# A grouped mixture-of-experts decoder kernel: the tokens' rows are gathered for two expert pairs at a time, between the weight units of gate and up, instead of for four pairs at once

## What is computed

```
def grouped_moe(h, w_router, router_bias, w_gate, w_up, w_down):
    scores = jax.nn.sigmoid((hf @ w_router).astype(jnp.float32))
    ...
    gates = jnp.sum(jax.nn.one_hot(expert_ids, N_EXPERTS, dtype=jnp.float32) * w_sel[..., None], axis=1)
    out = jnp.zeros_like(hf)
    for e in range(N_EXPERTS):
        y = (jax.nn.silu(hf @ w_gate[e]) * (hf @ w_up[e])) @ w_down[e]
        out = out + gates[:, e:e + 1] * y
    return out.reshape(b, s, d)
```

## Time and profile before

| | us |
|---|---|
| median of 3 runs | 651.88 (651.45 to 651.89) |
| span of the profiled execution, first to last instruction | 650.5 |
| device time around that span, if it is one of the runs shown | 1.0 to 1.4 |
| PE busy | 635.9 (98%) |
| PE's weight loads busy | 344.4 (53%) |
| DVE busy | 311.2 (48%) |
| ScalarE busy | 195.1 (30%) |
| GpSimd busy | 134.6 (21%) |
| loads of the weight ring (queue q1) | 234.46 MB, 85.4% of 16 DMA engines over the span |
| the 1024 matmuls of gate and up (L694) | 223.6 |
| the 512 of down (L715) | 113.8 |

### The profile page before, as it was taken

How to read it: one execution, slowest core, us unless ns; L and a number is a source line. 1 busy time by engine, 2 the same in 40 slices (tenths; PEclk the granted TensorE clock), 3 DMA queues, 4 the chain that set the end, 5 groups by cost and what they waited for, 6 DMA issues and landing times.

```text
span 650.5 us, 7970 instructions
## 1 busy us (share of the span) xinstructions
PE 635.9 (98%) x3227; PEld 344.4 (53%) x3227; DVE 311.2 (48%) x600; ACT 195.1 (30%) x389; POOL 134.6 (21%) x125
## 2 busy tenths in 40 slices
PE   8999999999999999999999999999999999999993
PEld 5887886453333443333488878764433344333431
DVE  6598997622033020320678989893032040320326
ACT  5832963240010221110193377351210032110111
POOL 1899300700000000000049960042000000000000
PEclk9999999999999999999999999999999999999998
DMA  8991299899999999999996118999999999999991
GB/s 360 433 391 66 102 430 428 358 434 422 430 426 426 432 425 427 427 427 429 427 426 297 50 66 316 430 368 418 429 431 424 430 426 425 430 424 431 427 391 67
DMA packets 18330, 240.79 MB, mean 370 GB/s; under 512 B 2032, under 2 KB 2160, under 8 KB 3440
## 3 DMA queue, kind: packets, MB, share of 16 engines
q1 hardware_dynamic: 17136, 234.46, 85.4%
q10 hardware_dynamic: 1152, 5.77, 2.2%
HBM read 239.17 MB, written 1.05 MB: 369 GB/s over the span
## 4 chain that ended last, share of the span: by engine, by line
PE 87%; DMA 5%; DVE 5%; issue 1%; ACT 1%; DVEq 0%
PE bank L694 31%; PE bank L715 16%; PE bank L586 13%; PE bank L743 5%; PE bank L560 5%; DMA ring<-in_units 5%; PE bank L667 2%; PE bank L805 2%; PE bank L817 2%; PE bank L647 2%; DVE w_split L1395 1%; PE bank L627 1%; PE bank L574 1%; PE bank L704 1%; PE bank L887 1%
## 5 line engine op out<-in xcount | busy, mean ns | idle before, releaser
L694 PE MATMUL bank<-ring,xe 128*64 128x512 f32 x1024 | 223.6, 593 | 0.6 <-DMA ring<-in_units 0.6
L694 PEld LDWEIGHTS bank<-ring,xe 128*64 128x64 f32 x1024 | 74.5, 137 | 143.1 <-issue 139.8
L715 PE MATMUL bank<-ring,area_b 128*64 128x512 f32 x512 | 113.8, 596 | 0.2
L1598 DVE TENSOR_TENSOR area_b<-area_b,bank 128x512 f32<-128x512 f32 x16 | 11.0, 688 | 209.4 <-PE bank L694 209.4
L1215 POOL TENSOR_TENSOR rstd<-var_eps,half_neg 128x1 f32<-128x1 f32 x18 | 10.6, 592 | 467.3 <-DVE var_eps L1327 467.3
L1248 POOL TENSOR_TENSOR in_lo<-ring,in_hi 128x512 fp32r<-128x512 f32 x56 | 71.2, 1328 | 13.6 <-ACT in_hi L1015 13.6
L715 PEld LDWEIGHTS bank<-ring,area_b 128*64 128x64 f32 x512 | 35.2, 137 | 66.7 <-issue 64.9
L1618 DVE SCALAR_TENSOR_TENSOR y_lo<-bank,slot_gate,y_hi 128x512 fp32r<-128x512 f32 x32 | 24.0, 751 | 85.0 <-ACT y_hi L1108 85.0
L1094 ACT ACTIVATE area_b<-bank 128x512 f32<-128x512 f32 x16 | 9.6, 597 | 163.8 <-PE bank L694 163.8
L1108 ACT ACTIVATE y_hi<-bank,slot_gate 128x512 fp32r<-128x512 f32 x32 | 22.0, 687 | 96.3 <-PE bank L715 96.3
L1675 DVE SCALAR_TENSOR_TENSOR bank<-mix,small,bank 128x256 f32<-128x256 f32 x116 | 45.6, 484 | 0.0
(11 more groups left out here) (204 smaller groups left out, 797.0 us busy)
## 6 DMA issues: line engine op xcount, KB each, us to landing
ring<-in_units SPq DMA_DIRECT2D x109, 2048.0 KB, 23.2
ln_par<-in_ln_rows ACTq DMA_DIRECT2D x4, 1024.0 KB, 8.4
ring<-in_units SPq DMA_DIRECT2D x2, 1024.0 KB, 8.2
h<-in_x SPq DMA_DIRECT2D x2, 512.0 KB, 4.2
piece_area<-in_branch_rows ACTq DMA_DIRECT2D x2, 512.0 KB, 5.5
ln_par<-in_ln_rows SPq DMA_DIRECT2D x1, 1024.0 KB, 36.1
piece_area<-in_sgw_cols ACTq DMA_DIRECT2D x2, 256.0 KB, 5.8
out<-h SPq DMA_DIRECT2D x1, 512.0 KB, 2.7
```

Of the source, the lines that this page charges most:

```text
L694: mm = pe.matmul(bank[2 + m][e * SLOTS:(e + 1) * SLOTS, :], xe[:, k, at + e * SLOTS:at + (e + 1) * SLOTS], w[:, c, m, e, :], start=k == 0, ...
L715: mm = pe.matmul(bank[5 + n][e * SLOTS:(e + 1) * SLOTS, :], hidT[:, k, e * SLOTS:(e + 1) * SLOTS], w[:, k, e, :], start=k == 0, stop=k == ...
```

## The change

`GROUP` goes from 4 to 2: all gathers are for two pairs (256 columns), so a layer has four of them, of 32 matmuls each. Two chunks share a PSUM bank.
- The first (`first_pairs`) stands where `first_pair` stood.
- The others stand inside the second pair of the group before (j = 1, 3, 5): chunks 0-1, 2-3 and 4-5 after the first, second and third unit of gate and up, chunks 6-7 inside down, ahead of its second unit.
- `combine` uses four banks (7, 4, 3 and 0 or 1), so its second half no longer waits for the first half's additions; it waits for those of the pair before.
- `turn_pick` moves ahead of `turn_hid`.
- On DVE the copy of `hidT` moves ahead of all four additions, and `picks` for the next group moves to the even pairs.
- The loads keep their order, their ring of 9 slots and their waits (the experts' third unit waits for the same count as the second, behind which it stands anyway).
- Tiles in `area_a` and `area_b` move; the `more` version follows.

The core of the diff:

```diff
-GROUP = 4
+GROUP = 2
-REST_BANKS = (1, 4, 7, 3, 1, 4, 7, 0)
-GROUP_BANKS = (2, 3, 0, 1, 4, 7, 0, 1)
-GATHERS = {"main": (3 * KC, 3 * TB), "more": (KC, TB)}
+NEXT_BANKS, MORE_BANKS = (0, 7, 4, 7), (0, 1, 7, 4)
+CHUNK_PAIRS = KC // 2
+GATHERS = {"main": (ITERS, ITERS), "more": (1, 1)}
-COMB_BANKS, LAST_COMB_BANKS = (7, 4, 7, 4), (7, 4, 2, 3)
+COMB_BANKS, LAST_COMB_BANKS = ((7, 4, 3, 0), (7, 4, 3, 1)), (7, 4, 2, 3)
...
+                def gather(g, p):
+
+                    dst = bank[(NEXT_BANKS if ps.main else MORE_BANKS)[p]]
+                    for c in (2 * p, 2 * p + 1):
+                        half = slice(c % 2 * GROUP * P, (c % 2 + 1) * GROUP * P)
                         for b in range(TB):
+                            wait_pick(g, b)
                             for part in (n_hi, n_lo):
+                                mm = pe.matmul(dst[:, half], part[:, b, c * P:(c + 1) * P], pick[:, b, :],
+                                               start=c % 2 == 0 and b == 0 and part is n_hi, stop=b == TB - 1 and part is n_lo,
+                                               skip_group_check=True)
+                    mm.then_inc(s["gathered"], 1)
...
                 def turn_pick(j):
 
                     nth("pick_w", j)
+                    if j >= 2:
+                        added(j - 2, 4)
...
                     for u in range(4):
-                        if j % GROUP == 0 and u == 2 and not (ps.main and j == 0):
-                            gather(g, range(4, KC))
...
+                            if j % GROUP == 0 and m == 0:
+                                wait_xe(g, k + 1)
+                            if j >= 2 and k == 0 and m == 1:
+                                added(j - 2, 3)
...
                         mm.then_inc(ps.used, 1)
+                        if gathers_next(j) and u < CHUNK_PAIRS - 1:
+                            if u == 0:
+                                nth("back", j - 1)
+                            elif j >= 2:
+                                added(j - 2, u)
+                            gather(g + 1, u)
...
                             if ps.main and j == pairs - 1 and n == 1 and k == 2:
                                 combine(j, (0, 1))
+                            if gathers_next(j) and n == 1 and k == 0:
+                                added(j - 1, 1)
+                                gather(j // GROUP + 1, CHUNK_PAIRS - 1)
...
-                        banks = LAST_COMB_BANKS if ps.main and j == pairs - 1 else COMB_BANKS
-                        if banks[k] == COMB_BANKS[k] and k >= 2:
-                            added(j, k - 1)
-                        elif k < 2 and j:
-                            added(j - 1, k + 3)
+                        banks = LAST_COMB_BANKS if ps.main and j == pairs - 1 else COMB_BANKS[j % 2]
+                        if k < 2 and j:
+                            added(j - 1, k + 1)
+                        if k < 2 and j + 1 < pairs and gathers_next(j + 1):
+                            wait_xe(j // GROUP + 1, 4 + 2 * k)
...
                     gate_up(j)
-                    if j == 0 and ps.main:
-                        other_pairs((0,))
-                        turn_pick(0)
-                        turn_hid(0)
-                        other_pairs((1,))
-                    elif j == 0:
-                        turn_pick(0)
-                        turn_hid(0)
-                    else:
+                    if j:
                         combine(j - 1, (0, 1))
-                        turn_hid(j)
+                    turn_pick(j)
+                    turn_hid(j)
+                    if j:
                         combine(j - 1, (2, 3))
-                        turn_pick(j)
                     down(j)
-                    if j == 0 and ps.main:
-                        other_pairs(range(2, KC))
-                    if (j + 1) % GROUP == 0 and j + 1 < pairs:
-                        gather((j + 1) // GROUP, range(0, 4))
...
+                tokens(0, range(CHUNK_PAIRS))
                 for j in range(pairs):
+                    gathers_next = ps.main and j % GROUP == GROUP - 1 and j + 1 < pairs
+                    if gathers_next:
+                        tokens(j // GROUP + 1, range(CHUNK_PAIRS - 1))
                     nth("gate_done", j)
                     act.activation(silu, bank[2][:, :], ACT.Silu).then_inc(s["silu"], 1)
...
                                        scale=slot_gate[:, j % 2:j % 2 + 1]).then_inc(s["y_hi"], 1)
+                        if gathers_next and n == 0:
+                            tokens(j // GROUP + 1, (CHUNK_PAIRS - 1,))
...
+                picks(0)
                 if ps.main:
-                    picks(0, 0, 2)
                     normal_low(l, 0)
                     normal_low(l, 1)
-                    picks(0, 2)
...
                     dve.tensor_tensor(hid, silu, bank[3][:, :], ALU.mult).then_inc(s["hid"], 1)
+                    nth("hid_t", j)
+                    dve.tensor_copy(hidT, bank[2][:, :].rearrange("p (c s) -> p c s", c=FC)).then_inc(s["hidT"], 1)
                     if ps.main and j == 1:
                         dve.wait_ge(acc_init, TB * (l + 1))
                     if j:
-                        add_back(j - 1, (0, 1))
-                    nth("hid_t", j)
-                    dve.tensor_copy(hidT, bank[2][:, :].rearrange("p (c s) -> p c s", c=FC)).then_inc(s["hidT"], 1)
-                    if j:
-                        add_back(j - 1, (2, 3))
+                        add_back(j - 1, range(4))
...
                     if j + 1 < pairs:
-                        if (j + 1) % GROUP == 0:
-                            picks((j + 1) // GROUP)
                         weighted_picks(j + 1)
+                        if j % GROUP == 0 and ps.main and j + GROUP < pairs:
+                            nth("pick_w", j + 1)
+                            picks(j // GROUP + 1)
```

More of the change, by code:

```diff
@@ L388, in __init__ @@
                 self.landed = landed_sems
-                self.chunks, self.picks = GATHERS[name]
+                self.gathers, self.picked = GATHERS[name]
         def moe_sems(name):
@@ L629, in first_pair @@
                                            skip_group_check=True)
-                            if b == TB - 1 and part is n_lo:
+                            if b == TB - 1 and part is n_lo and c % 2 == 1:
                                 mm.then_inc(s["gathered"], 1)
[L633 to L642, removed]
+                def gather(g, p):
+                    dst = bank[(NEXT_BANKS if ps.main else MORE_BANKS)[p]]
+                    for c in (2 * p, 2 * p + 1):
+                        half = slice(c % 2 * GROUP * P, (c % 2 + 1) * GROUP * P)
@@ L651, in gather @@
[L651 to L658, removed]
-                            added(GROUP * g - 2, 4)
-                        elif c == (3 if ps.main else 0) and g:
-                            nth("back", GROUP * g - 1)
-                            nth("slot_gate", GROUP * g - 1)
-                        for b in range(TB):
-                            if c == 0:
-                                wait_pick(g, b)
-                            for part in (n_hi, n_lo):
-                                mm = pe.matmul(bank[GROUP_BANKS[c] if ps.main else c % 2][:, :],
-                                               part[:, b, c * P:(c + 1) * P], pick[:, b, :],
-                                               start=b == 0 and part is n_hi, stop=b == TB - 1 and part is n_lo)
-                        mm.then_inc(s["gathered"], 1)
+                                mm = pe.matmul(dst[:, half], part[:, b, c * P:(c + 1) * P], pick[:, b, :],
+                                               start=c % 2 == 0 and b == 0 and part is n_hi, stop=b == TB - 1 and part is n_lo,
+                                               skip_group_check=True)
@@ L748, in experts @@
                 if ps.main:
-                    first_pair(n_hi)
-                    first_pair(n_lo)
-                else:
-                    gather(0, range(0, 4))
+                    first_pairs(n_hi)
+                    first_pairs(n_lo)
+                else:
+                    for p in range(CHUNK_PAIRS):
+                        gather(0, p)
                 for j in range(pairs):
@@ L1100, in experts @@
                        .then_inc(s["slot_gate"], 1)
-                    if ps.main and j == 0:
-                        tokens(0, (1,), 3 * P)
                     nth("slot_gate", j)
```

184 lines of the change are left out of this document (81 added, 103 removed).

## The result

The changed kernel takes 653.25 us (653.18 to 653.6, 8 runs) beside 651.69 (651.45 to 652.47, 8 runs) for the kernel before: ratio 1.0022, 95% interval 1.0012 to 1.0031. It is slower by 1.6 us. The forecast was 653.6, +1.7.

The account below looks back on a forecast made before the run. PE and DMA were taken to bound the experts within a microsecond per layer. PE's +0.07 + 3.45 - 6 x 0.30 = +1.7 at unit 45 became +1.15 and +0.6, together +1.7 on 651.9: 653.6 us, range 651.7 to 656.3.

Parts of the forecast that it names:

- Two limits within a microsecond: In the experts, PE loses only 0.26 and 0.81 us per layer to DMA at unit 45, so both limits nearly coincide.
- Insertions: Gathers placed into gate and up and down: 12 per layer at 0.958 + 0.375 us, net +3.45 us per layer.
- First gather: Ahead of unit 0, 32 matmuls of 256 instead of 128 columns: +0.07 us per layer.
- Middles: From the start of combine to the start of down: -0.30 us for each of seven middles per layer.
- The sum: PE +1.7 us at unit 45; +1.15 in the first layer, +0.6 in the second, together +1.7 us.
- At no cost: Picks, token copies, the additions behind hidT, new bank waits and loads: claimed to cost PE and the DMA stream nothing.
- B: Rival: the middles save only 0.15 us each, total +3.8 us, 655.7 us; chance 0.08.
- C: Rival: a new wait on PE at pairs with a gather, +4 us on top, 657 to 658 us; chance 0.03.
- D: Rival: gather matmuls of 256 columns take 0.14 instead of 0.12 us, +5 us, 658.7 us; chance 0.02.
- A: Rival: DMA stays the limit at unit 45, so not slower, 651.4 to 652.3 us; chance 0.42 with its border.

Follow-up runs that it names:

- before_light: The kernel before with three expert units per layer loaded to one eighth, so less DMA: 650.95 us, ratio 0.9986.
- mids_only: The kernel before with only the changed middles (four combine banks, turn_pick ahead of turn_hid, hidT copy ahead of the additions): 651.53 us, ratio 0.9995.
- mids_light: mids_only with three expert units per layer loaded to one eighth: 646.79 us, ratio 0.9921.
- merged_light: merged with three expert units per layer loaded to one eighth: 649.18 us, ratio 0.9953.
- old_dve: The changed kernel with the first two additions again ahead of the hidT copy on VectorE: 653.34 us, ratio 1.0020.
- old_pe: The changed kernel with turn_pick again behind the second half of combine: 653.13 us, ratio 1.0017.
- old_banks: The changed kernel with combine's two banks, their waits and VectorE's order as before, only turn_pick still ahead: 654.05 us, ratio 1.0027.
- after_light: The changed kernel with three expert units per layer loaded to one eighth: 653.30 us, ratio 1.0022.
- merged: The changed kernel with the three gathers inside gate and up made in a row behind the third unit: 652.09 us, ratio 1.0002.
- merged_early: merged with unit 9 loaded in two halves, the first once PE has used half of unit 0: 653.50 us, ratio 1.0021.

## Why the prediction was right

- **Two limits within a microsecond.** Right in both sizes: the stalls at unit 45 were 0.25 and 0.79 us (before_light), and PE time that comes is seen behind them: +1.63 - 0.25 = +1.38 and +1.63 - 0.79 = +0.84 in the stretches. The same fact made the saving of the middles invisible on the kernel before (mids_only against mids_light). One sentence of the prediction has it the wrong way round: with 3.96 us per unit against 4.93, PE is faster than the stream within the pairs. The stream begins with the ring full, and PE uses up that lead until unit 45.
- **Insertions.** 1.30 measured for 1.33. That the cost lies in the number of switches is shown by merged_light: the same matmuls, 12 switches fewer, -4.1 us, 0.34 out and back. That it is the change of column mode was only argued, as the type of the matmuls changes with it. The Trainium skill, "TensorEngine Tiling (Array Packing)", section Key Properties, says that changing the tiling mode drains the engine. These runs fit that and do not test it.
- **First gather.** Mis-sized: 0.28 instead of 0.07. The step was "The row of 128 columns is 3.76/32 = 0.1175 us each". That average contains the time for entering and leaving: 4.04 - 32 x 0.119 = 0.23 lies on top in the first gather after, and 3.76 - 32 x 0.111 = 0.21 before. L817's average over 48 matmuls, 0.1198, contains much less of it per matmul and was right for 256 columns. Start to start the step is 0.111 with 128 columns, so each matmul costs 0.008 more and not 0.0023. Like would have had to be compared with like.
- **Middles.** 0.28 to 0.33 for 0.30. The size was right and the reason half right: I gave it to the four banks and to the new orders on PE and VectorE together. Beside the four banks neither the copy's order (undone in old_dve) nor the place of turn_pick (undone in old_pe) is worth anything; the two were not undone together. Without the banks, turn_pick in front does nearly as much (old_banks).
- **The sum.** +1.63 at unit 45 for 1.7; then +1.38 - 0.28 = +1.10 and +0.84 - 0.28 = +0.56 for 1.15 and 0.6. Together +1.66, and the medians differ by 1.56. Errors of the first gather (+0.2 per layer) and of the insertions (12 x 0.03 = -0.4) partly cancelled, and that was luck. The spans of the two profiled executions differ by 1.0 only (650.5 and 651.5): the one before is some 0.66 us slower outside the stretches and the last middles, 0.32 of it ahead of the first gather. It was not one of the three runs shown: the changed kernel's profiled execution has 1.7 us around its span (653.22 for 651.5), which would make the one before about 652.2.
- **At no cost.** Held: after_light has the same stretch in both layers, and no row shows PE waiting for a gather's picks or banks, or for its tokens by more than the usual distance between two weight loads (0.3). Rivals B, C and D did not come about; A is what merged shows once 6 switches per layer are saved.

## What to carry to other kernels

When two resources are both nearly full, find the one place in a stage where they meet and read how much each has in hand there; that room, not the busy share, says how much of a gain or a loss is seen. Matmuls of another kind (here 128 columns in float32r amid 64 columns in float32) that are strewn into a stream cost PE by the number of their insertions, so put them in few places. A wait that could be taken away by more buffers can also be filled, as here, by moving an independent piece of the same engine into it.

## What the runs showed of the hardware

- A float32r matmul of 128 stationary and 256 moving columns, each with a new weight block, takes 0.119 us from one start to the next, one with 128 moving columns 0.111: halving the moving columns saves 7% there.
- Leaving the stream of 64-column float32 matmuls for 128-column float32r ones and coming back costs 0.34 us of TensorE, at a granted clock of 1.00. How much of it is the column mode and how much the type, no run shows.
- Issuing a 1 MB half of a load 1.7 us earlier, while another load was landing, moved the stream's bytes forward by 0.43 MB in 5 us and lost them again in the next 10. The kernel with it was 1.4 us slower (merged_early against merged), though the bytes moved by 300 us were the same.
